# Rows that all partitions share, stored to scratch and loaded back repeated, in place of products on TensorE

## The chip, the cores and the metric

One core of one Trainium2 chip. The metric is the device time of one launch in microseconds (us); a kernel is given by the median of its runs. TensorE is called PE here, VectorE DVE, ScalarE ACT, GpSimd POOL and SyncE SP, as in the profile.

## The reference, cut to what matters

Two blocks run one behind the other on 256 rows of 2048 numbers in float32, each with two layers. Nearly all of the arithmetic is products with large weights. The change touches two small places. In the first block each layer has a gated delta rule with 6 heads in chunks; its decay needs, for every pair (i, j) of a chunk, the difference of the summed gate at i and at j, and its keys are scaled by beta. In the second block the attention adds a relative bias per head.

```python
beta = jax.nn.sigmoid(b_raw)
gc = jnp.cumsum(g.reshape(bsz, n, CHUNK, H).transpose(0, 1, 3, 2), axis=-1)
decay = jnp.exp(jnp.where(incl, gc[..., :, None] - gc[..., None, :], -jnp.inf))
kb = kc * bc[..., None]
lower = jnp.where(strict, jnp.einsum('bhnid,bhnjd->bhnij', kb, kc) * decay, 0.0)
...
bias_rel = rel_bias.astype(F32)[t5_bucket(rel)].T
```

## The kernel before, in words

The program has one instruction stream per engine, written by five functions (`pe_program`, `act_program`, `dve_program`, `pool_program`, `sp_program`). PE, ACT and DVE walk the same list of weight chunks. A chunk is 512 columns wide and is worked off in tiles; a tile is 256 rows of weights (512 KB), which SP loads into one of three buffers RAW, ACT copies rounded to WH (L1339), DVE subtracts to get the rest WL (L1912), and PE multiplies in 12 products of 512 columns each (L731). ACT and DVE prepare the tile that stands four ahead of PE's (`split`, NW = 4).

Between two tiles each engine calls `pump`, which lets every small job that is in progress (a Python generator: `set_up`, `mixer_a`, `mixer_b`, `mixer_c`, the `leave_...` of the chunk before) write its instructions up to its next `yield`. So the place of small work in an engine's stream is counted in tiles, and an engine works its stream in order: an instruction that waits holds up the splitting of the weight tiles behind it. POOL is not in this walk; it issues the DMAs of small tensors and solves 32x32 blocks in `base`, each step behind its wait.

`set_up` (start of the program) makes the bias rows: one row per head, 512 wide, stretched over 128 partitions by a product (`row0` to `row7`), copied by DVE to BIASROW and stored by POOL to `bias_scratch`, 256 KB a head. The second block loads it from there. Only when `set_up` is through and the chunk `ba` has left PE does `mixer_c` begin. In `mixer_c`, BETA and GG (the gate) come out as 128 positions x 6 heads x 2 halves; PE sums the gate (`gs`), DVE copies the sums to GC. Then PE stretches GG's columns over all partitions and sums them (`dm0` to `dm2`, 12 products), DVE makes DT and XT from them (L2183, L2185), ACT takes the exponentials. Later PE stretches BETA (`kbm0` to `kbm2`, 12 products), DVE multiplies the keys by it into KB (`kb`, L2202), PE forms the products of keys (`kk`, `kq`), DVE writes LT (`lt`), and POOL's `base` starts when the last LT stands.

`mixer_b` adds two instructions of DVE (L2106) per tile for 60 tiles, and the chunks `qkv` bring a convolution of 12 DVE instructions (L2053). DT, LT and the upper part of BIASROW lie in the same memory AR, which is why the first DT instruction of layer 0 waits for `scr_in`, the landing of all eight bias stores.

Of the kernel before, what the change touches and what calls it, by code (L numbers as in the profile page):

```python
# [8 lines left out]
F32 = mybir.dt.float32  # L9
# [263 lines left out]
def program(nc, a, out):  # L273
    with ExitStack() as ctx:
# [32 lines left out]
        lt_scr = nc.dram_tensor("lt_scratch", [48, 32, 32], F32, kind="Internal")  # L307
        base_scr = nc.dram_tensor("base_scratch", [48, 32, 32], F32, kind="Internal")

        ident = C1[:, 0:128]  # L310
# [49 lines left out]
        for j, (mat, segs, width, row, kp) in enumerate(plan):  # L360
# [3 lines left out]
            else:  # L364
# [14 lines left out]
        R4, R3, R2 = range(4), range(3), range(2)  # L379
        u_pe = steps("setup_pe", ["prm0", "prm1", "prm5", "prm9"] + [f"row{h}" for h in range(8)])  # L380
        u_act = steps("setup_act", ["sin", "abs", "cos"])
        u_dve = steps("setup_dve", ["eps", "ones", "prm0", "prm1", "prm5", "prm9"] + [f"half{i}" for i in range(10)]
                      + ["pf", "an0", "an1", "kq0", "kq1", "kq2", "red0", "red1", "red2", "clip", "ab"]
                      + [f"row{h}" for h in range(8)])

# [26 lines left out]
        ca = ["bexp", "nea", "zab", "zexp", "ul", "edt0", "ext0", "edt1", "ext1", "edt2", "ext2", "nsq0"]  # L412
        cp_ = ["gs", "dm0", "dm1", "dm2"]
        cd = ["z", "b1", "beta", "u", "c0", "c1", "ur", "cu", "ce", "sp", "g", "gc", "xg"]
        for g in R3:
            cd += [f"dt{g}0", f"dt{g}1", f"xt{g}0", f"dt{g}2", f"dt{g}3", f"xt{g}1"]
# [4 lines left out]
        cp_ += [f"kbm{g}" for g in R3]  # L421
        cd += [f"kb{g}" for g in R3]
# [13 lines left out]

        i_lt, i_in, i_out, i_ttm = sem("lt_stored"), sem("base_in"), sem("base_stored"), sem("ttm_in")
        i_pool = steps("base_pool", per_layer(["zero"] + [f"{n}{j}" for j in range(1, 31) for n in ("mul", "add")] + ["one"]))

# [145 lines left out]
        HOT, RB = AR[0:32, 4096:4608], AR[0:32, 4608:4616]  # L585
        BIASROW = [AR[:, 5120 + 512 * h:5632 + 512 * h] for h in range(8)]
        lam0 = [0.8 - 0.6 * math.exp(-0.3 * l) for l in LL]


        Q = ar(0, 18, 256)  # L590
# [133 lines left out]
        def pe_program():  # L724
# [79 lines left out]
            def set_up():  # L804
                for _ in range(8):
                    yield
                T.wait_ge(prm_in, 16 * prm_loads)
                for i, g0 in enumerate((1, 5, 9)):
                    T.wait_ge(*p_gt.at(5 + i))
                    for g in range(g0, min(g0 + 4, groups)):  # L810
                        n = min(128, total - 128 * g)
                        o = STAGE + 128 * g
                        ins = tr(PS[:, 5 + i, 128 * (g - g0):128 * (g - g0) + n], AR[0:n, o:o + 128], n)
                    ins.then_inc(*u_pe(f"prm{g0}"))
                    yield
                e.flags.add("prm")
                yield
                yield
                T.wait_ge(hot_in, 32)
                T.wait_ge(*u_dve.at("prm9"))  # L820
                for h in range(8):
                    if h > 1:
                        T.wait_ge(*u_dve.at(f"row{h - 2}"))
                    mm(bank(4 + h % 2), RB[:, h:h + 1].broadcast_to([32, 128]), HOT).then_inc(*u_pe(f"row{h}"))
                    yield
                e.flags.add("set up")
# [92 lines left out]
            def mixer_c(l):  # L919
# [11 lines left out]
                yield  # L931
                for g in R3:
                    if g == 2:
                        T.wait_ge(*c_dve.at(m("xg")))
                    for p in R4:
                        hh, t = pair_of(g, p)
                        ins = mm(head((5, 6, 4)[g], p), GG[:, t, hh:hh + 1].broadcast_to([128, 128]), UINC)
                    ins.then_inc(*c_pe(m(f"dm{g}")))
                    if g > 0:
                        yield  # L940
                yield
# [4 lines left out]
                for r in range(6):  # L946
                    T.wait_ge(*c_act.at(m(f"nsq{r}")))
                    if r >= 3:
                        T.wait_ge(*c_act.at(m(f"nln{(r - 3) // 2}")))
                    else:  # L950
                        T.wait_ge(*c_dve.at(m("xt21")))
# [3 lines left out]
                for g in R3:  # L955
                    T.wait_ge(*c_act.at(m("nln2")))
                    for p in R4:
                        hh, t = pair_of(g, p)
                        ins = mm(head(4 + g, p), BETA[:, t, hh:hh + 1].broadcast_to([128, 128]), ident)
                    ins.then_inc(*c_pe(m(f"kbm{g}")))  # L960
                    yield
# [365 lines left out]
        def act_program():  # L1327
# [72 lines left out]
            def set_up():  # L1400
                for _ in range(11):
                    yield
                A.wait_ge(*u_dve.at("clip"))
                act(SINT, SM[:, 8:24], ACT.Sin).then_inc(*u_act("sin"))
                act(SM[:, 40:56], SM[:, 8:24], ACT.Abs).then_inc(*u_act("abs"))
                e.flags.add("prm")
                yield
                A.wait_ge(*u_dve.at("ab"))
                act(COST, SM[:, 40:56], ACT.Sin).then_inc(*u_act("cos"))
                yield  # L1410
                for h in range(8):
                    yield
                e.flags.add("set up")
# [31 lines left out]
            def leave_first(ch):  # L1445
# [28 lines left out]
                if n in conv4 + conv2:  # L1474
                    q0, w = 4 * int(n[3]), 4 if n in conv4 else 2
                    if l == 0:
                        A.wait_ge(*u_dve.at("row7" if n == "qkv4" else "half9"))
                    for c in range(w):
# [104 lines left out]
            def mixer_c(l):  # L1583
# [15 lines left out]
                act(Ef, Uf, ACT.Ln).then_inc(*c_act(m("ul")))  # L1599
                yield  # L1600
                yield
                yield
                yield
                for g in R3:
                    A.wait_ge(*c_dve.at(m(f"xt{g}1")))
                    act(DT[:, 4 * g:4 * g + 4, :], DT[:, 4 * g:4 * g + 4, :], ACT.Exp).then_inc(*c_act(m(f"edt{g}")))
# [291 lines left out]
        def dve_program():  # L1898
# [74 lines left out]
            def set_up():  # L1973
# [38 lines left out]
                yield  # L2012
                for h in range(8):
                    V.wait_ge(*u_pe.at(f"row{h}"))
                    cp(BIASROW[h], bank(4 + h % 2)).then_inc(*u_dve(f"row{h}"))
                    yield
                e.flags.add("set up")
# [121 lines left out]
            def mixer_c(l):  # L2139
# [33 lines left out]
                tt(XG, PS[:, 4, 16:22], GC[:, 0, :], SUB).then_inc(*c_dve(m("xg")))  # L2173
                yield
                V.wait_ge(*c_dve.at(m("xg")))
                if l == 0:
                    V.wait_ge(scr_in, 128)
                for g in R3:
                    V.wait_ge(*c_pe.at(m(f"dm{g}")))
                    for p in R4:  # L2180
                        hh, t = pair_of(g, p)
                        ps = head((5, 6, 4)[g], p)
                        stt(DT[:, 4 * g + p, :], ps, GC[:, t, hh:hh + 1], MINC, SUB, ADD).then_inc(*c_dve(m(f"dt{g}{p}")))  # L2183
                        if t == 1:
                            ts(XT[:, hh, :], ps, XG[:, hh:hh + 1], None, ADD).then_inc(*c_dve(m(f"xt{g}{p // 2}")))  # L2185
                    if g > 0:
                        yield
# [11 lines left out]
                for g in R3:  # L2199
                    V.wait_ge(*c_pe.at(m(f"kbm{g}")))  # L2200
                    V.wait_ge(*c_dve.at(m("nq5")))
                    tt(flat(KB[:, 2 * g:2 * g + 2, :]), flat(Q[:, 6 + 2 * g:8 + 2 * g, :]), bank(4 + g), MUL).then_inc(*c_dve(m(f"kb{g}")))  # L2202
                    yield
                for g in R3:
                    b, b2 = ((4, 5), (6, 4), (5, 6))[g]
                    dt = DT[:, 4 * g:4 * g + 4, :]
                    V.wait_ge(*c_act.at(m(f"ext{g}")))
                    V.wait_ge(*c_pe.at(m(f"kk{g}")))
                    stt(LT[:, 4 * g:4 * g + 4, :], by128(bank(b)), -1.0, dt, MUL, MUL).then_inc(*c_dve(m(f"lt{g}")))
                    V.wait_ge(*c_pe.at(m(f"kq{g}")))  # L2210
# [401 lines left out]
        def pool_program():  # L2612
# [10 lines left out]
            def narrow(phase, l, name):  # L2623
# [3 lines left out]
                G.dma_start(raw_view(j).rearrange("p (k n) -> p k n", k=kp), src).then_inc(narrow_in, 16)  # L2627

            def base(l):

# [28 lines left out]
            for l in LL:  # L2659
# [97 lines left out]
```

## Time and profile before

| | |
|---|---|
| median of 3 runs | 3398.24 us (3395.9 to 3400.61) |
| the profiled execution, its own time | 3400.07 us |
| its span | 3398.3 us |
| granted TensorE clock, mean | 0.994 |
| PE busy | 3311.2 us, 97% |
| DVE busy | 2243.7 us, 66% |
| ACT busy | 1825.8 us, 54% |
| POOL busy | 162.4 us, 5% |

The span runs from the first to the last instruction; the execution's own time has 1.77 us more around it. A busy share is a mean over stages with different limits, so each part of the change is to be read in its own stretch: `set_up` from 50 to 95 us, layer 0 of the first block up to about 590 us, layer 1 up to about 1090 us.

### The profile page before, as it was taken

Reading aid. Unit: us, or ns where it says so; the run is one execution under the profiler, and the core shown is the slowest. Engines: PE = TensorE matmul, PEld = TensorE weight load, DVE = VectorE, ACT = ScalarE, POOL = GpSimd, SP = SyncE. Lnnn points to the kernel's source line nnn. Section 1 sums busy time; section 2 is a strip of 40 time slices with the busy share of each in tenths; the row PEclk is TensorE's granted clock in tenths of the full one; section 3 lists DMA queues with packets and bytes.
Section 4 is the critical chain, followed back from the end, with each engine's and each line's share of the span. In section 5 each row is a group of like instructions: output and inputs, shape, how many; then the busy total and the mean of one; then the engine's idle time right before and its main releaser. Section 6 shows DMA issues by size and latency. Waiting matters only on the chain.

```text
span 3398.3 us, 40935 instructions
## 1 busy us (share of the span) xinstructions
PE 3311.2 (97%) x15842; PEld 2700.0 (79%) x15842; DVE 2243.7 (66%) x3056; ACT 1825.8 (54%) x2477; POOL 162.4 (5%) x243
## 2 busy tenths in 40 slices
PE   8999899999799999999999999999999999999998
PEld 6877678878588877888888888887778888888886
DVE  5887555986656676666666666665765666666666
ACT  4565645555645366555544544554665544455445
POOL 3023000042000000000000000000000000000000
PEclk9999999999999999999999999999999999999999
DMA  7544345544355555555556565655545655655564
GB/s 204 167 141 140 107 156 170 174 134 141 106 167 170 153 171 143 177 182 189 189 182 193 180 191 186 189 166 156 166 143 180 198 187 178 198 186 186 182 195 155
DMA packets 399761, 576.11 MB, mean 170 GB/s; under 512 B 25505, under 2 KB 222617, under 8 KB 399440
## 3 DMA queue, kind: packets, MB, share of 16 engines
q1 hardware_dynamic: 393344, 557.94, 53.1%
q0 software_dynamic: 5776, 14.39, 1.5%
q8 instruction: 125, 2.05, 0.3%
q10 hardware_dynamic: 448, 1.18, 0.1%
q14 instruction: 68, 0.56, 0.0%
HBM read 568.43 MB, written 4.98 MB: 169 GB/s over the span
## 4 chain that ended last, share of the span: by engine, by line
PE 82%; DVE 6%; ACT 5%; POOL 3%; DMA 3%; issue 2%; ACTq 0%; DVEq 0%
PE PS L731 79%; PE PS L728 3%; DVE WL L1912 2%; DMA RAW<-in_w_in 2%; POOL ZA L2650 1%; ACT WH L1339 1%; POOL SM L2647 1%; DVE AR L2053 1%; ACT AR L1713 0%; DVE ZA L2106 0%; ACT SM L1716 0%; DVE SM L2320 0%; DMA base_scratch<-ZA 0%; ACT AR L1720 0%; DVE AR L2318 0%
## 5 line engine op out<-in xcount | busy, mean ns | idle before, releaser
L1912 DVE TENSOR_TENSOR WL<-RAW,WH 128x1024 fp32r<-128x1024 f32 x1056 | 1295.0, 1231 | 878.8 <-ACT WH L1339 876.3
L1339 ACT ACTIVATE WH<-RAW 128x1024 fp32r<-128x1024 f32 x1056 | 1106.8, 1056 | 998.2 <-PE PS L731 625.1
L731 PE MATMUL PS<-WH,Ah 128*128 128x512 f32 x3520 | 1411.3, 401 | 11.6 <-DVE Al L1970 4.9
L731 PE MATMUL PS<-WL,Ah 128*128 128x512 f32 x3520 | 1377.1, 391 | 0.0
L731 PE MATMUL PS<-WH,Al 128*128 128x512 f32 x3520 | 1376.7, 391 | 0.0
L731 PEld LDWEIGHTS PS<-WH,Ah 128*128 128x128 f32 x3520 | 664.4, 189 | 170.6 <-issue 22.0
L731 PEld LDWEIGHTS PS<-WL,Ah 128*128 128x128 f32 x3520 | 664.0, 189 | 141.3
L731 PEld LDWEIGHTS PS<-WH,Al 128*128 128x128 f32 x3520 | 664.8, 189 | 138.1 <-issue 6.7
L731 PE MATMUL PS<-WH,Zh 128*128 128x512 f32 x704 | 278.6, 396 | 0.6
L731 PE MATMUL PS<-WL,Zh 128*128 128x512 f32 x704 | 274.6, 390 | 0.0
L731 PE MATMUL PS<-WH,Zl 128*128 128x512 f32 x704 | 274.1, 389 | 0.0
L731 PEld LDWEIGHTS PS<-WH,Zh 128*128 128x128 f32 x704 | 132.1, 188 | 35.1 <-DVE X L1922 9.1
L731 PEld LDWEIGHTS PS<-WL,Zh 128*128 128x128 f32 x704 | 132.2, 188 | 28.2
L731 PEld LDWEIGHTS PS<-WH,Zl 128*128 128x128 f32 x704 | 132.3, 188 | 26.3
L1922 DVE TENSOR_TENSOR X<-PS,X 128x1024 f32<-128x1024 f32 x104 | 126.9, 1221 | 35.2 <-PE PS L731 35.2
L731 PE MATMUL PS<-AR 64*128 64x128 f32 (+6 forms) x1184 | 130.2, 293 | 8.0 <-DVE AR L2318 5.2
L731 PEld LDWEIGHTS PS<-AR 64*128 64x128 f32 (+4 forms) x1184 | 107.2, 184 | 33.9 <-issue 12.5
L728 PE MATMUL PS<-C,AR 128*128 128x128 f32 (+2 forms) x610 | 86.4, 277 | 38.0 <-ACT AR L1720 23.0
L728 PEld LDWEIGHTS PS<-C,AR 128*128 128x128 f32 (+2 forms) x610 | 71.6, 142 | 58.3 <-DVE AR L2337 22.6
L2106 DVE SCALAR_TENSOR_TENSOR ZA<-ZA,PRM 128x226 f32<-128x226 f32 (+29 forms) x240 | 112.5, 510 | 0.0
L1420 ACT ACTIVATE AR<-PS,SM 128x512 f32<-128x512 f32 x104 | 65.8, 685 | 72.8 <-PE PS L731 72.7
L1420 ACT ACTIVATE ZA<-PS,SM 128x512 f32<-128x512 f32 (+1 forms) x88 | 54.5, 674 | 60.6 <-PE PS L731 51.0
(326 smaller groups left out, 2047.0 us busy)
## 6 DMA issues: line engine op xcount, KB each, us to landing
RAW<-in_w_in SPq DMA_DIRECT2D x368, 512.0 KB, 3.7
RAW<-in_w_up SPq DMA_DIRECT2D x704, 256.0 KB, 3.1
RAW<-in_w_down SPq DMA_DIRECT2D x176, 512.0 KB, 4.0
RAW<-in_w_out SPq DMA_DIRECT2D x64, 512.0 KB, 3.7
RAW<-in_w_o SPq DMA_DIRECT2D x64, 512.0 KB, 3.7
RAW<-in_w_in SPq DMA_DIRECT2D x64, 256.0 KB, 3.1
AR<-bias_scratch POOLq DMA_DIRECT2D x16, 192.0 KB, 4.8
X<-in_x SPq DMA_DIRECT2D x4, 512.0 KB, 7.9
```

The source lines that it names most:

```text
L728: return T.transpose(o, i, ident[0:n, 0:n])
L731: return T.matmul(o, lhs, rhs, start=start, stop=stop, skip_group_check=True)
L1339: act(WH[:, j % NW, 0:n], raw_view(j), ACT.Copy).then_inc(*w_hi())
L1420: act(dst[:, t, 0:n], PS[:, 2 * (ch.index % 2) + t, o:o + n], ACT.Copy, scale=RSTD[:, t:t + 1]).then_inc(*sems(names[t]))
L1912: tt(WL[:, j % NW, 0:w], raw_view(j), WH[:, j % NW, 0:w].bitcast(F32), SUB).then_inc(*w_lo())
L1922: tt(xs, PS[:, 2 * s:2 * s + 2, :], xs, ADD).then_inc(*x_added())
L2053: stt(Q[:, q0 + c, d:256], ptile(s, c)[:, 0:256 - d], P(("ccw", l), 18 * (3 - d) + q0 + c), Q[:, q0 + c, d:256], MUL, ADD).then_inc(*e_dve ...
L2106: stt(ACC[:, c, d:256], HB[:, c, 0:256 - d], P(("bcw", l), 4 * j + c), ACC[:, c, d:256], MUL, ADD).then_inc(*b_dve(m(f"t{j}_{c}")))
L2647: G.tensor_tensor(t, BASE[:, 0:j, j:j + 1].broadcast_to([48, j, n]), BASE[:, j:j + 1, j + 1:32].broadcast_to([48, j, n]), MUL).then_inc(*i ...
L2650: G.tensor_tensor(BASE[:, 0:j, j + 1:32], BASE[:, 0:j, j + 1:32], t, ADD).then_inc(*i_pool(m(f"add{j}")))
```

## The change

Bias: one product with all 8 heads as columns gives 8 rows of 512 on partitions 0 to 7; DVE copies them once; POOL stores each head with one DMA that reads the row of one partition 128 times. `set_up` has 7 steps fewer on PE, ACT and DVE. Beta and summed gate: POOL's new `rows` stores BETA and GC to `row_scratch` (two DMAs each, 128 x 6 numbers of 4 bytes) and loads each back with one DMA that repeats 6 KB on all 128 partitions, BETA to where LT will stand, GC to DT. The 24 products `dm` and `kbm` of a layer go; the steps that they stood in stay as empty steps. DVE makes DT and XT in place three tiles later than before, behind a wait for `decay_in`.

```diff
-                for h in range(8):
-                    if h > 1:
-                        T.wait_ge(*u_dve.at(f"row{h - 2}"))
-                    mm(bank(4 + h % 2), RB[:, h:h + 1].broadcast_to([32, 128]), HOT).then_inc(*u_pe(f"row{h}"))
-                    yield
+                mm(PS[0:8, 4, :], RB, HOT).then_inc(*u_pe("bias"))
+                yield
...
-                    for p in R4:
-                        hh, t = pair_of(g, p)
-                        ins = mm(head((5, 6, 4)[g], p), GG[:, t, hh:hh + 1].broadcast_to([128, 128]), UINC)
-                    ins.then_inc(*c_pe(m(f"dm{g}")))
...
-                    for p in R4:
-                        hh, t = pair_of(g, p)
-                        ins = mm(head(4 + g, p), BETA[:, t, hh:hh + 1].broadcast_to([128, 128]), ident)
-                    ins.then_inc(*c_pe(m(f"kbm{g}")))
...
-                for h in range(8):
-                    V.wait_ge(*u_pe.at(f"row{h}"))
-                    cp(BIASROW[h], bank(4 + h % 2)).then_inc(*u_dve(f"row{h}"))
-                    yield
+                V.wait_ge(*u_pe.at("bias"))
+                cp(BIASROW, PS[0:8, 4, :]).then_inc(*u_dve("bias"))
+                yield
...
                 tt(XG, PS[:, 4, 16:22], GC[:, 0, :], SUB).then_inc(*c_dve(m("xg")))
-                yield
+                for _ in R4:
+                    yield
                 V.wait_ge(*c_dve.at(m("xg")))
+                V.wait_ge(decay_in, 16 * (l + 1))
                 if l == 0:
                     V.wait_ge(scr_in, 128)
                 for g in R3:
-                    V.wait_ge(*c_pe.at(m(f"dm{g}")))
                     for p in R4:
                         hh, t = pair_of(g, p)
-                        ps = head((5, 6, 4)[g], p)
-                        stt(DT[:, 4 * g + p, :], ps, GC[:, t, hh:hh + 1], MINC, SUB, ADD).then_inc(*c_dve(m(f"dt{g}{p}")))
+                        dt = DT[:, 4 * g + p, :]
                         if t == 1:
-                            ts(XT[:, hh, :], ps, XG[:, hh:hh + 1], None, ADD).then_inc(*c_dve(m(f"xt{g}{p // 2}")))
+                            ts(XT[:, hh, :], dt, XG[:, hh:hh + 1], None, ADD).then_inc(*c_dve(m(f"xt{g}{p // 2}")))
+                        stt(dt, dt, GC[:, t, hh:hh + 1], MINC, SUB, ADD).then_inc(*c_dve(m(f"dt{g}{p}")))
...
-                    V.wait_ge(*c_pe.at(m(f"kbm{g}")))
+                    V.wait_ge(beta_in, 16 * (l + 1))
                     V.wait_ge(*c_dve.at(m("nq5")))
-                    tt(flat(KB[:, 2 * g:2 * g + 2, :]), flat(Q[:, 6 + 2 * g:8 + 2 * g, :]), bank(4 + g), MUL).then_inc(*c_dve(m(f"kb{g}")))
+                    tt(flat(KB[:, 2 * g:2 * g + 2, :]), flat(Q[:, 6 + 2 * g:8 + 2 * g, :]), flat(LT[:, 4 * g:4 * g + 4, :]),
+                       MUL).then_inc(*c_dve(m(f"kb{g}")))
...
+            def rows(l):
...
+                if l == 0:
+                    G.wait_ge(scr_in, 128)
+                else:
+                    G.wait_ge(*b_pe.at(f"{l - 1}.pw1"))
+                for i, (src, step, dst, landed_in) in enumerate(((BETA, "beta", LT, beta_in), (GC, "gc", DT, decay_in))):
+                    G.wait_ge(*c_dve.at(m(step)))
+                    for t in R2:
+                        G.dma_start(row_scr[l, i, :, 128 * t:128 * t + 128].rearrange("h p -> p h"), src[:, t, :],
+                                    allow_slow_non_contiguous=True).then_inc(row_out, 16)
+                    G.wait_ge(row_out, 32 * (2 * l + i + 1))
+                    G.dma_start(flat(dst), row_scr[l, i].rearrange("(o h) n -> o (h n)", o=1).broadcast_to([128, 1536])).then_inc(landed_in, 16)
...
                 if l == 0:
+                    G.wait_ge(*u_dve.at("bias"))
                     for h in range(8):
-                        G.wait_ge(*u_dve.at(f"row{h}"))
-                        G.dma_start(scr[h], BIASROW[h]).then_inc(scr_in, 16)
+                        G.dma_start(scr[h].rearrange("(o p) n -> o p n", o=1),
+                                    BIASROW[h:h + 1].unsqueeze(1).broadcast_to([1, 128, 512])).then_inc(scr_in, 16)
+                rows(l)
                 base(l)
```

POOL's stream in layer 0 after the change, with the semaphores that a row waits for: `scr_in` is the landing of the eight bias stores, `row_stored` that of the row stores, and the last row is the first step of `base`.

```order
L2668 DMA bias_scratch<-AR 128x1x512 [waits setup_dve]
L2668 DMA bias_scratch<-AR 128x1x512 x7
L2625 DMA row_scratch<-SM 128x6x1 [waits c_dve,scr_in]
L2625 DMA row_scratch<-SM 128x6x1
L2628 DMA AR<-row_scratch 128x1536 [waits row_stored]
L2625 DMA row_scratch<-SM 128x6x1 [waits c_dve]
L2625 DMA row_scratch<-SM 128x6x1
L2628 DMA AR<-row_scratch 128x1536 [waits row_stored]
L2638 DMA lt_scratch<-AR 32x12x32 [waits c_dve]
```

Before, the eight bias stores (each behind its own wait) were followed by the last row at once; six DMAs now stand between them, in four steps that each begin with a wait.

DVE's stream in layer 0 before the change, from the copy of the sums GC on; WL is the split of a weight tile, and the rows of L2183 are DT.

```order
L2171 COPY SM<-PS 128x12 [waits c_pe]
L2173 TENSOR_TENSOR SM<-PS,SM 128x6 [waits c_dve]
L2106 SCALAR_TENSOR_TENSOR ZA<-ZA,PRM 128x227 [waits b_dve] x2
L1912 TENSOR_TENSOR WL<-RAW,WH 128x1024 [waits w_hi]
L2183 SCALAR_TENSOR_TENSOR AR<-PS,SM,C 128x128 [waits c_pe,scr_in,c_dve]
L2183 SCALAR_TENSOR_TENSOR AR<-PS,SM,C 128x128
L2185 TENSOR_SCALAR AR<-PS,SM 128x128
```

The same engine after the change, the last two splits ahead of DT (L2167 and L2166 now).

```order
L2087 SCALAR_TENSOR_TENSOR ZA<-ZA,PRM 128x228 [waits b_dve] x2
L1894 TENSOR_TENSOR WL<-RAW,WH 128x1024 [waits w_hi]
L2087 SCALAR_TENSOR_TENSOR ZA<-ZA,PRM 128x229 [waits b_dve] x2
L1894 TENSOR_TENSOR WL<-RAW,WH 128x1024 [waits w_hi]
L2167 SCALAR_TENSOR_TENSOR AR<-AR,SM,C 128x128 [waits scr_in,decay_in,c_dve]
L2166 TENSOR_SCALAR AR<-AR,SM 128x128
L2167 SCALAR_TENSOR_TENSOR AR<-AR,SM,C 128x128 x2
```

Between GC and the first DT there was one split before, and there are four now. The first 12 of DT's and XT's 18 instructions stand ahead of the split that precedes the convolution of `qkv0`, and the last 6 directly behind that convolution; before, the last 6 stood one split behind the first 12, and three splits ahead of that convolution.

## Rows read from the trace of the kernel before

**Rows 1.** The page: busy time by engine, and the chain that ended last by engine.

```profile
PE 3311.2 (97%) x15842; PEld 2700.0 (79%) x15842; DVE 2243.7 (66%) x3056; ACT 1825.8 (54%) x2477; POOL 162.4 (5%) x243
...
PE 82%; DVE 6%; ACT 5%; POOL 3%; DMA 3%; issue 2%; ACTq 0%; DVEq 0%
```

**Rows 2.** Chain of waits in order of time: start us, us, what.

```profile
49.41 32.10 PE PS L731 x144
...
116.86 1.23 DVE WL L1912
...
119.96 4.68 DVE AR L2053 x12
...
194.78 23.86 PE PS L731 x130
...
223.35 1.87 POOL lt_scratch L2637 x3
...
537.53 21.81 PE PS L731 x96
...
619.23 4.67 DVE AR L2053 x12
```

**Rows 3.** POOL in order of time: start us, us, the issues of DMAs.

```profile
19.09 0.75 POOL L2616 DMA_DIRECT2D SM<-in_positions  x1
...
58.02 0.55 POOL L2667 DMA_DIRECT2D bias_scratch<-AR  x1 [27.98 <-DVE AR L2015]
```

**Rows 4.** DMA issues: out<-in, engine queue, count, KB each, median us to landing.

```profile
bias_scratch<-AR POOLq DMA_DIRECT2D x8, 256.0 KB, 2.6
...
base_scratch<-ZA POOLq DMA_DIRECT2D x2, 192.0 KB, 4.1
...
AR<-in_final_g ACTq DMA_DIRECT2D x1, 1024.0 KB, 6.5
...
SM<-in_positions POOLq DMA_DIRECT2D x1, 1.0 KB, 5.7
```

**Rows 5.** DMA queues, 25 to 130 us: packets, MB, share of 16 engines.

```profile
q1 hardware_dynamic: 7081, 13.64, 43.5%
q0 software_dynamic: 1232, 2.71, 12.7%
```

**Rows 6.** DVE in order of time, both layers: start us, us, line, out<-in.

```profile
57.04 0.68 DVE L2015 COPY AR<-PS 128x512 f32<-128x512 f32 x1
...
103.30 0.16 DVE L2171 COPY SM<-PS 128x12 f32<-128x12 f32 x1
...
106.56 0.61 DVE L2183 SCALAR_TENSOR_TENSOR AR<-PS,SM,C 128x128 f32<-128x128 f32 x2 [1.04 <-PE PS L731]
...
109.67 0.81 DVE L2106 SCALAR_TENSOR_TENSOR ZA<-ZA,PRM 128x227 f32<-128x227 f32 x2
...
210.52 0.68 DVE L2202 TENSOR_TENSOR AR<-AR,PS 128x512 f32<-128x512 f32 x1
...
602.00 0.17 DVE L2171 COPY SM<-PS 128x12 f32<-128x12 f32 x1 [0.57 <-PE PS L731]
...
616.14 1.23 DVE L1912 TENSOR_TENSOR WL<-RAW,WH 128x1024 fp32r<-128x1024 f32 x1 [1.11 <-ACT WH L1339]
```

**Rows 7.** PE in order of time: start us, us, line, out<-in.

```profile
54.82 1.12 PE L731 MATMUL PS<-AR 32*128 32x512 f32 x2
...
58.81 1.12 PE L731 MATMUL PS<-AR 32*128 32x512 f32 x2
...
85.25 0.50 PE L731 MATMUL PS<-WH,Ah 128*128 128x512 f32 x1 [1.82 <-ACT ZA L1485]
...
201.22 1.05 PE L731 MATMUL PS<-C,SM 128*128 128x128 f32 x8
...
204.86 1.05 PE L731 MATMUL PS<-C,SM 128*128 128x128 f32 x8
...
212.16 1.95 PE L731 MATMUL PS<-AR 128*128 128x128 f32 x16
```

More of the change, by code:

```diff
@@ L308, in program @@
         base_scr = nc.dram_tensor("base_scratch", [48, 32, 32], F32, kind="Internal")
+        row_scr = nc.dram_tensor("row_scratch", [2, 2, 6, 256], F32, kind="Internal")
         ident = C1[:, 0:128]
@@ L379, in program @@
         R4, R3, R2 = range(4), range(3), range(2)
-        u_pe = steps("setup_pe", ["prm0", "prm1", "prm5", "prm9"] + [f"row{h}" for h in range(8)])
+        u_pe = steps("setup_pe", ["prm0", "prm1", "prm5", "prm9", "bias"])
         u_act = steps("setup_act", ["sin", "abs", "cos"])
         u_dve = steps("setup_dve", ["eps", "ones", "prm0", "prm1", "prm5", "prm9"] + [f"half{i}" for i in range(10)]
-                      + ["pf", "an0", "an1", "kq0", "kq1", "kq2", "red0", "red1", "red2", "clip", "ab"]
-                      + [f"row{h}" for h in range(8)])
+                      + ["pf", "an0", "an1", "kq0", "kq1", "kq2", "red0", "red1", "red2", "clip", "ab", "bias"])
         def per_layer(names):
@@ L412, in program @@
         ca = ["bexp", "nea", "zab", "zexp", "ul", "edt0", "ext0", "edt1", "ext1", "edt2", "ext2", "nsq0"]
-        cp_ = ["gs", "dm0", "dm1", "dm2"]
+        cp_ = ["gs"]
         cd = ["z", "b1", "beta", "u", "c0", "c1", "ur", "cu", "ce", "sp", "g", "gc", "xg"]
         for g in R3:
-            cd += [f"dt{g}0", f"dt{g}1", f"xt{g}0", f"dt{g}2", f"dt{g}3", f"xt{g}1"]
+            cd += [f"dt{g}0", f"xt{g}0", f"dt{g}1", f"dt{g}2", f"xt{g}1", f"dt{g}3"]
         for r in range(6):
@@ L420, in program @@
             cd += [f"nq{r}"]
-        cp_ += [f"kbm{g}" for g in R3]
         cd += [f"kb{g}" for g in R3]
@@ L437, in program @@
         i_lt, i_in, i_out, i_ttm = sem("lt_stored"), sem("base_in"), sem("base_stored"), sem("ttm_in")
+        row_out, beta_in, decay_in = sem("row_stored"), sem("beta_in"), sem("decay_in")
         i_pool = steps("base_pool", per_layer(["zero"] + [f"{n}{j}" for j in range(1, 31) for n in ("mul", "add")] + ["one"]))
@@ L585, in program @@
         HOT, RB = AR[0:32, 4096:4608], AR[0:32, 4608:4616]
-        BIASROW = [AR[:, 5120 + 512 * h:5632 + 512 * h] for h in range(8)]
+        BIASROW = AR[0:8, 5120:5632]
         lam0 = [0.8 - 0.6 * math.exp(-0.3 * l) for l in LL]
@@ L931, in mixer_c @@
                 yield
-                for g in R3:
-                    if g == 2:
-                        T.wait_ge(*c_dve.at(m("xg")))
-                    for p in R4:
-                        hh, t = pair_of(g, p)
-                        ins = mm(head((5, 6, 4)[g], p), GG[:, t, hh:hh + 1].broadcast_to([128, 128]), UINC)
-                    ins.then_inc(*c_pe(m(f"dm{g}")))
-                    if g > 0:
-                        yield
+                yield
+                yield
                 yield
@@ L950, in mixer_c @@
                     else:
-                        T.wait_ge(*c_dve.at(m("xt21")))
+                        T.wait_ge(*c_dve.at(m("xg")))
                     mm(bank(NB[r]), ONES[:, :], NS[r]).then_inc(*c_pe(m(f"nsum{r}")))
@@ L954, in mixer_c @@
                 yield
-                for g in R3:
-                    T.wait_ge(*c_act.at(m("nln2")))
-                    for p in R4:
-                        hh, t = pair_of(g, p)
-                        ins = mm(head(4 + g, p), BETA[:, t, hh:hh + 1].broadcast_to([128, 128]), ident)
-                    ins.then_inc(*c_pe(m(f"kbm{g}")))
+                for _ in R3:
                     yield
@@ L1410, in set_up @@
                 yield
-                for h in range(8):
-                    yield
+                yield
                 e.flags.add("set up")
@@ L1476, in leave_first @@
                     if l == 0:
-                        A.wait_ge(*u_dve.at("row7" if n == "qkv4" else "half9"))
+                        A.wait_ge(*u_dve.at("bias" if n == "qkv4" else "half9"))
                     for c in range(w):
@@ L1599, in mixer_c @@
                 act(Ef, Uf, ACT.Ln).then_inc(*c_act(m("ul")))
[L1600 to L1603, printed above, removed]
+                for _ in range(7):
+                    yield
                 for g in R3:
-                    A.wait_ge(*c_dve.at(m(f"xt{g}1")))
+                    A.wait_ge(*c_dve.at(m(f"dt{g}3")))
                     act(DT[:, 4 * g:4 * g + 4, :], DT[:, 4 * g:4 * g + 4, :], ACT.Exp).then_inc(*c_act(m(f"edt{g}")))
@@ L2012, in set_up @@
                 yield
-                for h in range(8):
-                    V.wait_ge(*u_pe.at(f"row{h}"))
-                    cp(BIASROW[h], bank(4 + h % 2)).then_inc(*u_dve(f"row{h}"))
-                    yield
+                V.wait_ge(*u_pe.at("bias"))
+                cp(BIASROW, PS[0:8, 4, :]).then_inc(*u_dve("bias"))
+                yield
                 e.flags.add("set up")
@@ L2173, in mixer_c @@
                 tt(XG, PS[:, 4, 16:22], GC[:, 0, :], SUB).then_inc(*c_dve(m("xg")))
-                yield
+                for _ in R4:
+                    yield
                 V.wait_ge(*c_dve.at(m("xg")))
+                V.wait_ge(decay_in, 16 * (l + 1))
                 if l == 0:
@@ L2208, in mixer_c @@
                     V.wait_ge(*c_pe.at(m(f"kk{g}")))
+                    V.wait_ge(*c_dve.at(m("kb2")))
                     stt(LT[:, 4 * g:4 * g + 4, :], by128(bank(b)), -1.0, dt, MUL, MUL).then_inc(*c_dve(m(f"lt{g}")))
@@ L2627, in narrow, with m @@
                 G.dma_start(raw_view(j).rearrange("p (k n) -> p k n", k=kp), src).then_inc(narrow_in, 16)
+            def rows(l):
+                def m(s):
+                    return f"{l}.{s}"
+                if l == 0:
[9 more added lines that the diff above has]
+                    G.dma_start(flat(dst), row_scr[l, i].rearrange("(o h) n -> o (h n)", o=1).broadcast_to([128, 1536])).then_inc(landed_in, 16)
             def base(l):
```

## Prediction

> **What bounds the kernel now.** I read the page first: PE is busy 97% of the span, and the chain that ended last is PE's for 82%, DVE's for 6% [rows 1]. That is a mean over stages, so I then followed the chain in order of time through the places that the change touches [rows 2]. The reader is to see four things there. From 49.4 to 81.5 us, in `set_up`, the chain is 144 products of PE in one piece: a product taken away there is time. From about 117 us it is DVE: the split at 116.86, then the convolution at 119.96. At 194.78 it is PE again, and at 223.35 POOL, which waits for LT. In layer 1 PE leads at 537.53, DVE at the convolution of 619.23. An undisturbed tile is 96 products / 12 = 8 tiles in 21.81 us, 2.73 us each. What starts the convolution of layer 0 later than 119.96 therefore comes through to the end undiminished: the chain never leaves that line of work for one with slack.
>
> **The new stores.** POOL issues its first bias store at 58.02, 0.55 us each [rows 3]. The one copy of the new kernel can stand at about the same time, so the issues begin there too. Each store still moves 256 KB, but reads one partition where it read 128. No row of before does that, so I bound it. Below: as now, 2.6 us from issue to landing, 101 GB/s. The store of `base_scratch` reads fewer partitions (48 blocks) and takes 4.1 us for 192 KB, 48 GB/s [rows 4]: the rate falls as the source gets narrower. Above: what one of the 16 DMA engines carries, as if one partition were read by one engine. Between 25 and 130 us the weight queue moves 13.64 MB in 43.5% of 16 engines' 105 us, 731 us, so 18.7 GB/s, and 256 KB would take 14.0 us; POOL's queue 2.71 MB in 213 us, 12.7 GB/s and 20.6 us [rows 5]. I take 10 us (26 GB/s), between 48 and 18.7 GB/s and nearest to the latter. All eight are on one queue, so one behind the other: `scr_in` is complete at S = 58 + 80 = 138, where before it stood long before DVE came to it.
>
> The Trainium skill, "SBUF — State Buffer", section "Door 1: The DMA port swizzle (why `[64,N]` ≈ `[32,N]`)", says that partitions 0 to 3 go through one port at 27.6 GB/s. By that, as an estimate, a store takes 9.5 us and eight take 76, and the sum below would be about +51 us; no row of before shows it.
>
> **The row stores and loads behind them.** POOL's `rows(0)` begins with `scr_in`. A wait is answered in 0.30 us: DVE's copy of row 0 ends at 57.04 + 0.68 and POOL's issue begins at 58.02 [rows 3, 6]. A small issue costs 0.75 [rows 3], two of them 1.5. The landing of a 1 KB transfer takes 5.7 us [rows 4]; that is the lower bound, since a row store has 768 pieces of 4 bytes. At POOL's present 213 us / 1232 packets = 0.173 us [rows 5], 768 packets on 16 engines are 8.3 us, two stores 16.6: the upper bound. I take 8.3 for the pair, because small pieces should be quicker than those of 2 KB. The load repeats 6 KB on 128 partitions, 768 KB: between 2.6 us for 256 KB and 6.5 for 1 MB [rows 4], 5.5. Beta: 0.3 + 1.5 + 8.3 + 0.3 + 0.55 = 10.95, and its load lands unwaited for. GC behind it: 1.5 + 8.3 + 0.3 + 0.55 + 5.5 = 16.15. So `decay_in` comes 27.1 us after S, T = 165. Bounds: 22 and 44 us after S.
>
> **The wait on DVE.** Before, DVE copied GC at 103.30 and went on to DT at 106.56 after 1.04 us of waiting for PE; the 12 instructions of the first two groups lasted until 109.67, 3.1 us, with no wait for `scr_in` [rows 6]. After, DVE comes to DT at about 108, right behind the split that ended at 118.09 (116.86 + 1.23) less what PE gains below, and stands until T. Behind that instruction in its stream are all later splits WL and the steps of L2106; PE has four tiles ready, 11 us of work, and stops; ACT and SP stop when their buffers are full. From T the way to the convolution is 3.1 us of DT and XT and 1.87 us (118.09 to 119.96: the last split and its step), so T + 4.98 = 170 against 119.96: +50.0. Six DT instructions, another 1.55 us, now stand behind the convolution: +51.6.
>
> **What is saved.** A step of `set_up` with its row product takes 58.81 − 54.82 = 3.99 us, 1.26 more than a tile [rows 7]. Of the seven that go, one lies in PE's wait for ACT that ends at 85.25 (1.82 us) and saves nothing; the other six save 6 × 1.26 = 7.5 us. The 7 DVE copies of 0.68 [rows 6] save nothing, as DVE waits for PE there. `dm` goes: three groups, each 3.64 − 2.73 = 0.91 (201.22 to 204.86 for the like groups of `kbm`) [rows 7], 2.7 us, on PE's way to DVE. Together 10.2 us: but all of it before the wait, so it only makes DVE stand earlier. `kbm` is another 2.7 us, but the products of keys at 212.16 [rows 7] wait for DVE's last KB, which ends at 210.52 + 0.68 = 211.20 [rows 6] and costs the same from AR as from PSUM: 1.0 us is gained. ACT's exponentials three tiles later cost nothing: DVE uses them only in LT, after 212, and if that cover were gone it would be the 3 tiles, 8 us. The load of BETA lands at about S + 17 = 155, its first use is behind the convolution.
>
> **Layer 1.** GC stands at 602.17 [rows 6], `scr_in` no longer counts, and POOL's beta is done long before. `decay_in`: 602.17 + 0.3 + 16.15 = 618.6. DVE arrives behind its split at 616.14 + 1.23 less `dm`'s 2.7, 614.6 [rows 6]: it waits 4.0, the convolution is at 618.6 + 4.98 = 623.6 against 619.23 [rows 2], +4.4; with 1.55 and −1.0, +4.9.
>
> **Sum.** 51.6 − 1.0 + 4.9 = +55.5. The profiled execution took 3400.07 us of its own, 1.8 more than the median of the runs, so 3455.6 for a like execution and 3454 for the median. No row of before has PE standing for 50 us; should its clock come back at the lower level, the first tiles take up to twice 2.73 us, but DVE leads there, so I put it at nothing.
>
> **Rivals.** *Stores as quick as before, the not-slower case.* Then S = 58 + 8 × 2.6 = 79, and T hangs on GC: 103.46 − 7.5 + 0.3 + 16.15 = 112.4, the convolution at 117.4, −2.6. With 1.55 − 1.0 + 4.9 the sum is +2.9, 3401; with the lower bound of the row stores it is −2.3 (2.6 less in each layer), 3396. The store is a mere copy of equal bytes, which speaks for it; the 48 GB/s of the narrower one speaks against. It decides at T = 116.3 (the sum is then 0.2%, 6.8 us, about what a measurement can tell from no change), S = 89, 3.9 us a store. Chance 0.23.
> *Two stores at a time.* If the slow thing is the source partition and the queue works on two rows at once, S = 58 + 40 = 98, T = 125, the convolution at 130, +10 + 5.5 = +15.6: 3414. For it: in 25 to 130 us the queues use 56% of the engines, so there is room [rows 5]. Against: one queue. Chance 0.14. (The same page of the Trainium skill puts partitions 4 to 7 on another port; if both ran side by side S would be 96 and the sum about +13.5. No row shows it.)
> *One partition is slower.* At 14 us S = 170, T = 197, the sum +87.6, 3486; at 20.6 us S = 223, +140, 3538. Chance 0.13.
> *My forecast*, stores of 8 to 12 us (+39.5 to +71.5, so 3438 to 3470), has 0.46; 0.04 is left for what I don't see, as weights and stores robbing each other.
>
> **How the numbers follow.** The time is that of the forecast, 3454. The quick stores with dear row stores, and two at a time, lie below it; to leave out no more than 2 in 10 the range goes from 3394, which holds nearly all of the quick case, to 3488, which takes in 14 us a store. Faster by over 0.2% needs quick stores and cheap row stores and a gain not counted: 0.05. Within 0.2%: the rest of the quick case, 0.20. Slower: 0.75.
>
> **What would show it.** DMA issues: bias stores 2.6 us before; each landing alone, or in the queue, tells S, and the first `row_scratch` issue on POOL should stand at 138. DVE: one idle stretch from about 108 to 165 ahead of the first DT, ended by a DMA; if it is under 10 us, the stores were quick. PE: idle from some 11 us after DVE stops. Layer 1: about 4 us of waiting before DT; 1.4 us if the row stores cost 5.7. `kk` directly behind KB. The forecast is wrong if the first `row_scratch` issue stands before 95 or after 165, or if DT waits and the convolution is late but PE, by its four tiles and a later stretch with slack, gives part of it back.

## The result, and the profile after

The changed kernel takes 3476.70 us (median of 4 runs, 3474.83 to 3482.05); the kernel before took 3397.12 in its runs beside it. The ratio is 1.0232, 95% interval 1.022 to 1.0245: 79.6 us slower. 3454 was predicted, with 3394 to 3488 as the range. Direction, range and the price of a store held. The way from the store to the lost time did not: the prediction has DVE wait for the stores, and in the trace the weight tiles starve beside them.

The page of the changed kernel, busy time and chain by engine (before: [rows 1]):

```profile
PE 3305.5 (95%) x15732; PEld 2695.0 (78%) x15732; DVE 2238.6 (64%) x3049; ACT 1825.8 (53%) x2477; POOL 169.6 (5%) x255
...
PE 80%; DVE 7%; ACT 5%; DMA 5%; issue 2%; POOL 2%; another core or an unknown queue 1%; ACTq 0%; DVEq 0%; POOLq 0%
```

DMA has grown from 3% to 5% of the chain, and an unknown queue has come in with 1%. The chain of waits in order of time says where (start us, us, what):

```profile
58.15 43.85 DMA RAW<-in_w_in
...
102.04 31.60 another core or an unknown queue
...
140.40 4.43 PE PS L731 x12
...
149.10 9.02 DMA row_scratch<-SM
...
159.78 13.16 DMA row_scratch<-SM
173.22 6.19 DMA AR<-row_scratch
...
184.34 4.68 DVE AR L2034 x12
...
659.23 10.41 DMA row_scratch<-SM
671.32 12.28 DMA row_scratch<-SM
683.88 5.67 DMA AR<-row_scratch
694.50 4.67 DVE AR L2034 x12
```

Where PE led from 49 to 82 us in [rows 2], the chain now stands on a weight tile, 43.85 us for a load that took a median of 3.6 to 4.4 us before. Behind it comes a piece with no name. ACT's stream shows what it is: both are waits for RAW, a buffer that a weight tile is loaded into (start us, us, line, out<-in, idle time ahead and what ended it):

```profile
102.02 1.06 ACT L1324 ACTIVATE WH<-RAW 128x1024 fp32r<-128x1024 f32 x1 [40.77 <-DMA RAW<-in_w_in]
133.66 1.06 ACT L1324 ACTIVATE WH<-RAW 128x1024 fp32r<-128x1024 f32 x1 [30.59 <-DMA RAW<-in_w_in]
```

Two weight tiles in 72 us, where PE works one off in 2.73. The stores explain it, as the run with the bias part alone will show. `bias_scratch`, its eight issues (ns of one, first and last start) and their landing:

```profile
L2668 POOL DMA_DIRECT2D bias_scratch<-AR x8: 522/523/542, 57.3 to 60.9; - x8
...
DMA to landing us min/median/max: 11.7/43.4/72.9
```

The last store lands at 60.9 + 72.9 = 133.8, when the tiles come back. Eight stores in 133.8 − 57.3 = 76.5 us are 9.56 us each, 27.4 GB/s. The queues from 57 to 134 us (packets, MB, share of 16 engines; [rows 5] for before):

```profile
q0 software_dynamic: 640, 2.10, 87.7%
q1 hardware_dynamic: 945, 1.83, 6.1%
```

The stores hold 88% of the engines' time: 0.877 x 77 x 16 / 640 = 1.69 us for a packet, as a mean that has very small ones in it; a full packet of 4 KB takes 2.28 us (worked out below). A weight packet takes 0.061 x 77 x 16 / 945 = 0.08 us, but only 1.5 of them pass for each packet of the stores. That fits what the Trainium skill says in "DMA: Bandwidth & Descriptors", section "Queues, rings and completion order": an engine takes turns between its queues packet by packet. A queue of slow packets would then slow the others to its own pace. The runs below, with quicker packets in the stores, bear it out: the tiles get quicker with them.

What follows is on DVE (idle time ahead in brackets):

```profile
103.10 1.23 DVE L1894 TENSOR_TENSOR WL<-RAW,WH 128x1024 fp32r<-128x1024 f32 x1 [41.47 <-ACT WH L1324]
134.75 1.23 DVE L1894 TENSOR_TENSOR WL<-RAW,WH 128x1024 fp32r<-128x1024 f32 x1 [30.42 <-ACT WH L1324]
...
147.43 0.23 DVE L2131 RECIPROCAL SM<-SM 128x12 f32<-128x12 f32 x1
...
156.75 0.17 DVE L2152 COPY SM<-PS 128x12 f32<-128x12 f32 x1 [0.58 <-PE PS L731]
...
179.49 0.35 DVE L2167 SCALAR_TENSOR_TENSOR AR<-AR,SM,C 128x128 f32<-128x128 f32 x1 [2.29 <-DMA AR<-row_scratch]
```

DVE loses its 72 us at splits WL without data, not at DT, where it waits 2.29. PE has one wait of 61.5 us there:

```profile
135.92 1.97 PE L728 MATMUL PS<-C,ZA 128*128 128x128 f32 x8 [61.52 <-ACT ZA L1404]
```

BETA (the reciprocal) is done at 147.66 and GC (the copy) at 156.92; before, GC was there at 103.46 [rows 6]. Only then can the rows start, on POOL:

```profile
148.24 1.71 POOL L2625 DMA_DIRECT2D row_scratch<-SM  x2 [86.81 <-DVE SM L2131]
158.40 0.56 POOL L2628 DMA_DIRECT2D AR<-row_scratch  x1 [8.45 <-DMA row_scratch<-SM]
158.95 1.65 POOL L2625 DMA_DIRECT2D row_scratch<-SM  x2
173.22 0.56 POOL L2628 DMA_DIRECT2D AR<-row_scratch  x1 [12.62 <-DMA row_scratch<-SM]
```

POOL's first row store waits for BETA, not for `scr_in`, and GC's store begins 2.0 us after GC because POOL still stood at BETA's. While PE stands, the granted clock falls (stretches in us; busy us and instructions of PE, PEld, DVE, ACT, POOL, then granted clock, DMA share, GB/s):

```profile
103.00:134.00 31.00, 0.00 (x0) 0.00 (x0) 1.23 (x1) 0.41 (x2) 0.00 (x0) 0.50 0.91 62
134.00:180.00 46.00, 34.24 (x140) 27.89 (x141) 22.04 (x42) 24.17 (x36) 4.47 (x6) 0.80 0.72 157
```

0.50 is the level of 1.2 GHz: PE had done nothing for the whole stretch.

### The profile page after: what moved, and what is told of

It reads as the page before. It is cut to its first block, busy times and chain, and to the rows that moved or that the text cites. A ratio compares the mean times of both kernels' runs of the same rounds, so it can differ in the third digit from the quotient of the medians.

```text
span 3473.0 us, 40722 instructions
## 1 busy us (share of the span) xinstructions
PE 3305.5 (95%) x15732; PEld 2695.0 (78%) x15732; DVE 2238.6 (64%) x3049; ACT 1825.8 (53%) x2477; POOL 169.6 (5%) x255
## 4 chain that ended last, share of the span: by engine, by line
PE 80%; DVE 7%; ACT 5%; DMA 5%; issue 2%; POOL 2%; another core or an unknown queue 1%; ACTq 0%; DVEq 0%; POOLq 0%
PE PS L731 77%; PE PS L728 3%; DVE WL L1894 2%; DMA RAW<-in_w_in 2%; ACT WH L1324 1%; DMA row_scratch<-SM 1%; POOL ZA L2651 1%; DVE AR L2034 1%; DVE ZA L2087 1%; POOL SM L2648 1%; ACT AR L1695 0%; DMA AR<-row_scratch 0%; ACT SM L1698 0%; DVE SM L2304 0%
## 5 line engine op out<-in xcount | busy, mean ns | idle before, releaser
L731 PE MATMUL PS<-WH,Ah 128*128 128x512 f32 x3520 | 1414.9, 402 | 23.4 <-DVE WL L1894 14.4
L731 PE MATMUL PS<-AR 64*128 64x128 f32 (+6 forms) x1170 | 122.5, 289 | 11.7 <-DVE AR L2302 5.1
L728 PE MATMUL PS<-C,ZA 128*128 128x128 f32 x304 | 41.3, 281 | 70.4 <-ACT ZA L1404 70.4
```

What stands on the lines that cost most here:

```text
L728: return T.transpose(o, i, ident[0:n, 0:n])
L731: return T.matmul(o, lhs, rhs, start=start, stop=stop, skip_group_check=True)
```

## The experiments

All are named by what differs; us are medians where several runs were made, and the kernel before, run beside them, stood at 3400.01 for the first four and 3398.16 for the others.

**The bias as before, the rows as after.**

```diff
-                mm(PS[0:8, 4, :], RB, HOT).then_inc(*u_pe("bias"))
+                for h in range(8):
...
+                    mm(bank(4 + h % 2), RB[:, h:h + 1].broadcast_to([32, 128]), HOT).then_inc(*u_pe(f"row{h}"))
...
-                                    BIASROW[h:h + 1].unsqueeze(1).broadcast_to([1, 128, 512])).then_inc(scr_in, 16)
+                        G.dma_start(scr[h], BIASROW[h]).then_inc(scr_in, 16)
```

> The bias rows are made and stored as before the change (8 products, 8 copies, stores that read 128 partitions); beta and the summed gate go by rows as in the changed kernel. Theory (the stores that read one partition hold the DMA engines, the weight tiles starve behind them, and PE stops): the stores land in about 2.6 us each again, no weight tile takes over 12 us between 58 and 95 us, GC stands at about 103. What is left is the rows: beta at 94, its store 10 us, GC's store 13, the load 6, so the convolution of layer 0 at about 130 against 119.96, +10, and layer 1 +11: 3418 (3410 to 3426). Rival (the waits of DVE for the rows are the loss, and the stores are hidden): at least 3455.

3426.52, ratio 1.0081 (1.0066 to 1.0096): 26.5 us slower than before, just above the expected range and far from the rival's 3455. The stores land as they used to:

```profile
L2674 POOL DMA_DIRECT2D bias_scratch<-AR x8: 540/540/547, 55.9 to 89.9; - x8
...
DMA to landing us min/median/max: 2.3/2.5/4.6
```

The convolution of layer 0 is at 130.7, +10.8 as expected, but layer 1 cost another 15 in place of 11: its convolution is at 645.17 against 619.15. In layer 1 there are no bias stores, yet the weight tiles are slow there too. DMA issues from 607 to 642 us (count, KB each, median us to landing):

```profile
RAW<-in_w_in SPq DMA_DIRECT2D x8, 512.0 KB, 10.4
AR<-row_scratch POOLq DMA_DIRECT2D x2, 768.0 KB, 8.8
row_scratch<-SM POOLq DMA_DIRECT2D x4, 3.0 KB, 10.1
```

Before, in the like stretch (596 to 625 us):

```profile
RAW<-in_w_in SPq DMA_DIRECT2D x8, 512.0 KB, 3.6
```

So the row stores hurt twice: POOL's chain is long, and the weights go short beside it. Which of stores and loads does that, the run with rows by head tells.

**The bias alone.** The kernel before with the bias part of the diff only; `dm`, `kbm` and DT as before.

> Only the bias part of the change; beta and the summed gate are stretched by PE as before. Theory (stores hold the DMA engines, weights starve): the last store lands at about 134 us, PE stands from about 73 to 134, GC comes at about 157 and the convolution 16.7 us later, at 173 against 119.96: +53, 3450 (3440 to 3458); layer 1 is as before. Rival (the waits for the rows are the loss): 7 us faster than before, 3390.

3453.04, ratio 1.0161 (1.0144 to 1.0178): +53.0, as expected. No DVE instruction waits for rows here, so the rival falls: the bias part alone costs 53 us, at the splits:

```profile
102.17 1.23 DVE L1907 TENSOR_TENSOR WL<-RAW,WH 128x1024 fp32r<-128x1024 f32 x1 [41.46 <-ACT WH L1335]
133.91 1.23 DVE L1907 TENSOR_TENSOR WL<-RAW,WH 128x1024 fp32r<-128x1024 f32 x1 [30.52 <-ACT WH L1335]
```

The convolution of layer 0 is at 173.1, +53.2, and that is all of it. The two parts, 53.0 and 26.5, add up to 79.5, and the whole is 79.6.

**Four copies of each row, on neighbours or spread.** DVE repeats the columns of RB, so that the one product makes four copies of a row; the second kernel has the copies in the other order.

```diff
-                mm(PS[0:8, 4, :], RB, HOT).then_inc(*u_pe("bias"))
+                mm(PS[0:32, 4, :], RBX, HOT).then_inc(*u_pe("bias"))
...
+                cp(RBX.rearrange("p (h j) -> p h j", j=4), RB.unsqueeze(2).broadcast_to([32, 8, 4])).then_inc(*u_dve("rbx"))
...
-                                    BIASROW[h:h + 1].unsqueeze(1).broadcast_to([1, 128, 512])).then_inc(scr_in, 16)
+                                    BIASROW[4 * h:4 * h + 4].unsqueeze(1).broadcast_to([4, 32, 512])).then_inc(scr_in, 16)
```

> As the changed kernel, but the one bias product makes four copies of each row, on four neighbouring partitions (4h to 4h+3), and a head's store reads each of the four 32 times. If the price is that of a group of four neighbouring partitions, a store still takes 9.5 us and the time is that of the changed kernel, 3477 (3470 to 3484). If it is the price of each single partition, a store takes about 2.5 us and the time is about 3412. If it is the destination or the repeated reading, 3477 too.

> As the run with four neighbours, but the four copies of a row stand on partitions h, 8+h, 16+h and 24+h. If neighbours share a price, the four copies are now in four groups and a store takes about 2.5 us: 3412 (3404 to 3420). If each single partition has its price, 3412 as well. If the destination or the repeated reading of one source is the price, 9.5 us a store and 3477.

3424.54 and 3424.42, one run each: the same. Neighbours first, spread second:

```profile
L2670 POOL DMA_DIRECT2D bias_scratch<-AR x8: 680/681/719, 54.8 to 59.6; - x8
...
DMA to landing us min/median/max: 4.4/13.4/23.1
```

```profile
L2670 POOL DMA_DIRECT2D bias_scratch<-AR x8: 680/681/722, 57.5 to 62.3; - x8
...
DMA to landing us min/median/max: 4.5/12.4/23.7
```

From the first issue to the last landing that is (59.6 + 23.1 − 54.8) / 8 = 3.49 us a store with neighbours and (62.3 + 23.7 − 57.5) / 8 = 3.56 spread, where one copy took 9.56. The destination and the 256 KB are the same, so neither is the price. The time lies between the two that were expected, because these are means over stores that run side by side, which the expectations left out. The packets of POOL's queue tell it. From 60 to 66 us in the changed kernel:

```profile
q0 software_dynamic: 41, 0.17, 97.4%
```

With neighbours from 57 to 58.5, and from 60 to 66:

```profile
q0 software_dynamic: 10, 0.04, 25.6%
...
q0 software_dynamic: 142, 0.58, 96.5%
```

Spread from 59.3 to 59.9, with the count of all packets, and from 62 to 66:

```profile
DMA packets 49, 0.09 MB, mean 157 GB/s; under 512 B 17, under 2 KB 17, under 8 KB 49
...
q0 software_dynamic: 31, 0.06, 30.3%
...
q0 software_dynamic: 110, 0.45, 98.2%
```

The single partition of the changed kernel gives 28 GB/s and keeps all 16 engines at it, 0.974 x 6 x 16 / 41 = 2.28 us for a packet of 4 KB. The first store with neighbours takes a quarter of the engines: 10 packets of 4 KB in 1.5 us are 27 GB/s, and a packet takes 0.61 us. So four neighbours together give no more than one partition alone. The first spread store has about as many engines, and its 31 − 17 = 14 packets of 4 KB in 0.6 us are 96 GB/s, 0.21 us a packet. The price is that of a group of four neighbouring partitions. The two runs take the same time because four stores are soon under way at once: with neighbours each on a group of its own (97 GB/s together), spread all on the same four groups (113 GB/s together). That a store has four engines here and all 16 in the changed kernel is read from these shares; what decides it was not tested.

A tile still took a median of 11.9 us (neighbours) and 17.7 (spread) from 57 to 85 us, where it was 56.5 in the changed kernel from 57 to 134, and the rows' part had been counted with 11 us in layer 1, so 3412 was too low.

**Sixteen copies**, spread over all partitions, each read 8 times.

> As the changed kernel, with 16 copies of each bias row on partitions h, 8+h, ..., 120+h, each read 8 times. One copy took 9.6 us a store, four 3.5 (neighbours or spread). If each single partition has its price, 16 copies are no longer bound by it: 2.6 us a store or less, the last landing some 21 us after the first issue, and the time about 3418, between the run with the bias as before (3426.5) and that less the row products (3419). If the many pieces of the repeated form are the price in the runs with four copies, a store still takes 3.5 us and the time stays 3424.

3417.21, one run, where about 3418 was expected.

```profile
L2670 POOL DMA_DIRECT2D bias_scratch<-AR x8: 544/552/559, 57.5 to 61.1; - x8
...
DMA to landing us min/median/max: 3.9/6.2/9.2
```

(61.1 + 9.2 − 57.5) / 8 = 1.6 us a store, and a tile from 57 to 85 us takes a median of 5.1 us. The 16 copies of a row stand in 16 groups of four neighbours. With 1, 4 and 16 groups read at a time a store takes 9.56, 3.5 and 1.6 us on the mean. The time is about that of the kernel with the rows alone, less the row products (3426.5 − 7.5 = 3419).

**One small store, repeated from DRAM.** The 8 rows are stored once; eight transfers from DRAM to DRAM repeat them, and beta's row store and DT wait for the small store only.

```diff
+                    G.dma_start(one_scr[:, :], BIASROW).then_inc(bias_out, 16)
+                    G.wait_ge(bias_out, 16)
                     for h in range(8):
-                        G.dma_start(scr[h].rearrange("(o p) n -> o p n", o=1),
-                                    BIASROW[h:h + 1].unsqueeze(1).broadcast_to([1, 128, 512])).then_inc(scr_in, 16)
+                        G.dma_start(scr[h], one_scr[h:h + 1].broadcast_to([128, 512])).then_inc(scr_in, 16)
```

> As the changed kernel, but the 8 bias rows are stored once (16 KB) to a small scratch, and eight transfers from DRAM to DRAM repeat them into bias_scratch; beta's row store and DT wait for the small store only. Theory (reading one partition holds the DMA engines): no partition is read 128 times, so the repeats take about 3 us each and take no more from the weights than the 128-partition stores of before; what is left is the rows' part, measured as +26 where the bias was as before, less the 7.5 us of row products that are gone: +15 to +22 against the kernel before. Rival (128 reads of one and the same row are slow wherever they come from): weights starve again, +55 to +80.

> Only the bias part, in the form with the small store and the repeats from DRAM to DRAM; beta and the summed gate are stretched by PE as before. Theory: the row products that are gone are all that remains, 7 us faster than before (5 to 8 us; ratio 0.9976 to 0.9986). If the repeats from DRAM rob the weights as one partition did: +50.

With the rows as after: 3418.02, ratio 1.0058 (1.0044 to 1.0071), +19.9. With the bias alone: 3394.43, ratio 0.9987 (0.9978 to 0.9996), 3.7 us faster than before by the medians, where 5 to 8 were expected; the interval, 1.4 to 7.5 us, holds both. Reading one row 128 times costs no time that shows when it comes from DRAM: each of the eight transfers has landed at most 10.9 us after its issue. In the second kernel GC of layer 1 stands at 595.46 where it stood at 602.00 [rows 6], 6.5 us earlier, and the span of the profiled execution is 3390.8 against 3398.3. That is the row products' worth in this one execution, which is among the quicker of its ten.

**Rows by head.** As the kernel with the small store and the rows, but PE makes beta and the summed gate with the heads on partitions (two products each), so that a row store is 6 pieces of 1 KB; the gate goes first.

```diff
+                for t in R2:
+                    mm(PS[0:6, 4, 128 + 128 * t:256 + 128 * t], GG[:, t, :], UINC)
...
+                for t in R2:
+                    ins = mm(PS[0:6, 5, 128 * t:128 + 128 * t], BETA[:, t, :], ident)
...
-                    for t in R2:
-                        G.dma_start(row_scr[l, i, :, 128 * t:128 * t + 128].rearrange("h p -> p h"), src[:, t, :],
-                                    allow_slow_non_contiguous=True).then_inc(row_out, 16)
+                    G.dma_start(row_scr[l, i], ROWS[0:6, i, :]).then_inc(row_out, 16)
```

> As the run with the small bias store, but beta and the summed gate come out of PE by head: two products each (6 partitions x 128), copied by DVE to 6 rows of 256 and stored with one DMA of 6 x 1 KB in place of 2 x 768 pieces of 4 bytes; the gate goes first. Theory (the row stores' small pieces cost 10 to 13 us each on POOL's chain and rob the weight tiles, which took 10.1 us in place of 3.6): a store lands in 3 us, the decay row is there about 11 us after GC, when DVE comes to it, weight tiles take under 5 us, and the sum is -7.5 (row products) -2 (kbm) +1 (copies) +0 to 4: 5 to 9 us faster than before (ratio 0.9975 to 0.9988). Rival (the loads that repeat 6 KB on 128 partitions rob the weights, not the stores): the loss of some +20 stays, 15 or more slower than before.

3393.56, ratio 0.9986 (0.9977 to 0.9995): 4.6 us faster than before where 5 to 9 were expected, the fastest by its median, though not to be told from the bias alone with the small store. DVE in layer 1 (compare the 2.6 us of waiting for rows that the changed kernel has there):

```profile
597.00 0.17 DVE L2159 COPY SM<-PS 128x12 f32<-128x12 f32 x1 [1.20 <-PE PS L733]
...
609.35 0.35 DVE L2177 SCALAR_TENSOR_TENSOR AR<-AR,SM,C 128x128 f32<-128x128 f32 x1
```

and its DMA issues from 592 to 627 us:

```profile
RAW<-in_w_in SPq DMA_DIRECT2D x9, 512.0 KB, 3.8
AR<-row_scratch POOLq DMA_DIRECT2D x2, 768.0 KB, 5.5
row_scratch<-AR POOLq DMA_DIRECT2D x2, 6.0 KB, 4.3
```

The loads of 768 KB are the same, and the tiles are back at 3.8 us. The run with the small store, which differs from this one only in how the rows are made, stored and ordered, has in the like stretch (606 to 632 us):

```profile
RAW<-in_w_in SPq DMA_DIRECT2D x4, 512.0 KB, 10.1
```

So the stores of 4-byte pieces robbed the tiles, not the loads. DT waits for nothing. How much of the gain is the shape of the store and how much the gate's going first was not taken apart by a run; in the changed kernel POOL came 1.7 us late to the gate in layer 0 and 3.5 in layer 1 (158.95 against GC at 156.92, 670.49 against 666.67, each less the 0.3 in which a wait is answered).

## Why the prediction was right, and where it was not

| step | predicted | measured |
|---|---|---|
| a one-partition store | 10 us, one behind the other | 9.56 us, one behind the other |
| the last one lands, S | 138 | 133.8 |
| BETA after S | long done | 13.9 us after S |
| rows, from there to `decay_in` | 27.1 us | 31.8 us |
| T, `decay_in` of layer 0 | 165 | 179.4 |
| T to the convolution | 4.98 us | 4.9 us |
| convolution of layer 0 | +50.0 | +64.4 |
| layer 1 (with what stands between) | +5.5 | +10.9 |
| sum | +55.5 | +74.7 in the span |

The table is of the profiled execution, which was the quickest of the four runs (3474.83, against 3400.07 for the one before); the medians lie 79.6 apart.

**What bounds the kernel.** Right: what was late at the convolution came through. It was +64.4 us late, POOL's first LT store +65.1 (288.48 against 223.35), the convolution of layer 1 +75.3, the end +74.7.

**The stores.** Right in price, order and S. The estimate of 9.5 us from the Trainium skill's 27.6 GB/s ("SBUF — State Buffer", section "Door 1: The DMA port swizzle (why `[64,N]` ≈ `[32,N]`)") was met within 1%, and the stores of partitions 4 to 7 did not run beside those of 0 to 3. The Trainium skill gives that rate to partitions 0 to 3 together, and the runs with four copies agree: 28 GB/s from one partition, 27 from four neighbours, 96 from four in different groups.

**The wait on DVE.** This step failed, though its number came near: +64.4 against +50.0. It took the stores for a thing that delays `scr_in` alone, with DVE and PE at work up to DT, at 108. The stores in fact held the DMA engines, and the weight tiles starved: DVE stood at the splits from 62 us on, PE from about 74 (its one wait there is 61.5 us long). The prediction had "weights and stores robbing each other" among what it did not see, at 0.04. The two accounts agree up to S, since both stop until then. They differ in what is done by S: in the prediction BETA and GC are, in the trace the program still has the tiles ahead of BETA to work off, 13.9 us. With −4.2 from S and +4.7 from the rows that is the whole difference at T: −4.2 + 13.9 + 4.7 = 14.4. That the time stayed inside the range is in part luck: S, which both accounts share, makes most of the loss, and the range had been widened for slower stores, not for starving tiles.

**The rows.** Mis-sized by 4.7 us: the first stores and their wait took 10.2 us (148.24 to 158.40), the gate's 14.3 (158.95 to 173.22), the load 6.2. 8.3 us was taken for a pair of stores; the bounds 5.7 and 16.6 hold the measured ones.

**Layer 1.** Mis-sized: "POOL's beta is done long before" was wrong. POOL came to the gate's store 3.8 us after GC, the store took 13.4 us, and `decay_in` was 23 us after GC, not 16.45; the tiles beside it took 10.1 us, for which nothing was counted.

**What is saved.** The 7.5 us of the row products are borne out in part: 3.7 by the medians with the bias alone (interval 1.4 to 7.5), 6.5 at GC of layer 1 in its profile, and 6.6 by the medians between the rows with the small store and the rows with the bias as before, whose intervals overlap. In the changed kernel they lie inside the stall. That `dm` and `kbm` are worth something is not shown: the kernel with rows by head has neither and is no faster than the one that keeps both.

**The clock** was put at nothing. It fell to the lower level while PE stood; the tile after the stall took 4.43 us for 12 products, 1.7 more than an undisturbed one, and stands in the chain to BETA. But before, the tile after the short wait that ended at 85.25 took as long (4.33) and is in the chain too, so hardly anything of it is due to the change. No further cost was seen.

**The rivals.** Quick stores would have given some +20 us, not +3: the runs with small or 16-copy stores have just that, because the rows' part alone is +26.5, and some +20 where the row products are gone. The case counted DVE's wait alone, and not the weights that the row stores hold up.

## What to carry to other kernels

A DMA's cost is not only when it lands: look at what its packets take on the 16 engines that the weight stream shares, by the queue's share and packet count, before calling a background transfer hidden. Here a row that everybody needs was cheap to repeat from DRAM, or from copies in many groups of four partitions, and dear from one partition or from four neighbours. And a mean time per transfer says little of one transfer as long as it isn't known how many run side by side. Before a small tensor is stored in 4-byte pieces, let the engine that makes it lay it out with the long side along a partition; here that took four products and two copies a layer, with the gate's store put first, and the loss of 20 us was gone.

## What was not expected of the hardware

Reading one partition went at 27.4 GB/s with all 16 engines at it, and four neighbours went no faster (27 GB/s with a quarter of the engines), where four partitions in different groups gave 96. The stores that read four partitions ran four at a time. Eight stores from one partition each, 2.1 MB, brought the weight stream down to 1.83 MB in 77 us, where it moved 13.64 MB in 105 us before [rows 5]. Pairs of row stores of 3 KB each, as 4-byte pieces, took 9 to 13 us, and beside them 512 KB tiles took 10.1 us in place of 3.6.
